# Latent attention in a one-core encoder trunk: query products behind half a projection block, one weight block split on VectorE, projection products ahead of a value product

## The reference

```python
h = x @ w_in
c_q, c_kv, k_rope, dq, dk, dv = jnp.split(h, offs, axis=-1)
q = (rms_norm(c_q, g_q, RMS_EPS) @ w_uq).reshape(b, s, MLA_HEADS, MLA_NOPE_DIM + MLA_ROPE_DIM)
kv = (rms_norm(c_kv, g_kv, RMS_EPS) @ w_ukv).reshape(b, s, MLA_HEADS, MLA_NOPE_DIM + MLA_V_DIM)
...
o_mla = mla_attention(q_nope, q_rope, k_nope, k_rope, v_mla)      # softmax(q k^T) v, per head
o_d = diff_attention(dq[..., 0, :], dq[..., 1, :], dk[..., 0, :], dk[..., 1, :], dv, lam)
```

## Time and profile before

| | |
|---|---|
| median of three runs | 792.22 us (792.11 to 793.13) |
| the profiled execution | 793.97 us |
| its span | 791.9 us |
| busy: PE, PEld | 739.6 us (93%), 614.2 us (78%) |
| busy: DVE, ACT, POOL | 581.1 us (73%), 483.8 us (61%), 269.8 us (34%) |
| granted TensorE clock, mean | 0.975 of full |
| DMA | 179.35 MB, 226 GB/s over the span |

### The profile page before, as it was taken

How to read it: one execution, slowest core, us unless ns; L and a number is a source line. 1 busy time by engine, 2 the same in 40 slices (tenths; PEclk the granted TensorE clock), 3 DMA queues, 4 the chain that set the end, 5 groups by cost and what they waited for, 6 DMA issues and landing times.

```text
span 791.9 us, 12710 instructions
## 1 busy us (share of the span) xinstructions
PE 739.6 (93%) x3844; PEld 614.2 (78%) x3844; DVE 581.1 (73%) x974; ACT 483.8 (61%) x874; POOL 269.8 (34%) x292
## 2 busy tenths in 40 slices
PE   4999989998999699999999899999999999999984
PEld 3898878887888477777788677888877777777862
DVE  6965354556554766686677889998998888888757
ACT  3334354556554656675045267887878888888635
POOL 3132356556654243334421114232222222222111
PEclk9999999999999879999997999999999999999998
DMA  9724310222024863202835759999999999999863
GB/s 342 250 104 134 119 54 27 81 67 67 2 95 155 286 246 120 94 27 80 297 137 200 284 177 392 392 381 388 385 364 382 379 383 365 391 380 375 287 212 159
DMA packets 71484, 179.35 MB, mean 226 GB/s; under 512 B 11687, under 2 KB 28071, under 8 KB 71444
## 3 DMA queue, kind: packets, MB, share of 16 engines
q1 hardware_dynamic: 66692, 166.34, 55.5%
q0 software_dynamic: 4752, 12.51, 6.4%
HBM read 153.20 MB, written 30.42 MB: 232 GB/s over the span
## 4 chain that ended last, share of the span: by engine, by line
PE 57%; DMA 20%; DVE 12%; ACT 5%; issue 3%; POOL 2%; SPq 1%; DVEq 0%; ACTq 0%; POOLq 0%
PE bank L648 33%; DMA rawG<-in_w_gate 16%; PE bank L1774 3%; PE bank L1776 3%; PE bank L1775 3%; DVE eGl L1929 2%; DMA dv_l<-dv_low 2%; PE bank L783 2%; PE bank L1797 1%; PE bank L1796 1%; PE bank L1795 1%; PE bank L2154 1%; ACT eGh L1859 1%; DVE eUl L1929 1%; DVE eDl L1929 1%
## 5 line engine op out<-in xcount | busy, mean ns | idle before, releaser
L1929 DVE TENSOR_TENSOR eDl<-rawD,eDh 128x1024 fp32r<-128x1024 f32 x68 | 80.2, 1220 | 12.6 <-ACT eDh L1859 12.4
L1268 POOL TENSOR_SCALAR me<-me,mrec 128x512 f32<-128x512 f32 (+1 forms) x48 | 64.8, 1354 | 55.9 <-DVE mrec L1447 55.8
L1929 DVE TENSOR_TENSOR eUl<-rawU,eUh 128x1024 fp32r<-128x1024 f32 x68 | 78.8, 1220 | 2.7 <-ACT eUh L1859 2.7
L1929 DVE TENSOR_TENSOR eGl<-rawG,eGh 128x1024 fp32r<-128x1024 f32 x64 | 75.5, 1221 | 6.1 <-ACT eGh L1859 5.1
L2052 POOL DMA_INDIRECT acc_rows<-yg,idx_s x16 | 29.7, 1859 | 133.6 <-ACT yg L1884 133.6
L1859 ACT ACTIVATE eGh<-rawG 128x1024 fp32r<-128x1024 f32 x64 | 65.9, 1059 | 7.6 <-DMA rawG<-in_w_gate 7.1
L1859 ACT ACTIVATE eDh<-rawD 128x1024 fp32r<-128x1024 f32 x64 | 64.0, 1056 | 0.0
L1774 PE MATMUL bank<-eGh,xgT_h 128*128 128x512 f32 x136 | 56.0, 412 | 8.6 <-DVE xgT_l L1934 7.4
L1859 ACT ACTIVATE eUh<-rawU 128x1024 fp32r<-128x1024 f32 x64 | 62.9, 1052 | 0.0
L1774 PE MATMUL bank<-eUh,xgT_h 128*128 128x512 f32 x136 | 54.6, 401 | 0.0
L1776 PE MATMUL bank<-eGl,xgT_h 128*128 128x512 f32 x136 | 53.3, 392 | 0.0
(11 more groups left out here) (345 smaller groups left out, 2186.0 us busy)
## 6 DMA issues: line engine op xcount, KB each, us to landing
rawG<-in_w_gate SPq DMA_DIRECT2D x68, 512.0 KB, 15.6
rawU<-in_w_up SPq DMA_DIRECT2D x68, 512.0 KB, 12.3
rawD<-in_w_down SPq DMA_DIRECT2D x68, 512.0 KB, 13.6
wb_raw<-in_w_in SPq DMA_DIRECT2D x8, 512.0 KB, 4.7
wo_raw<-in_w_o SPq DMA_DIRECT2D x8, 512.0 KB, 7.4
xln_rows<-res SPq DMA_DIRECT2D x6, 512.0 KB, 3.8
dqk_high<-st_h SPq DMA_DIRECT2D x8, 384.0 KB, 2.3
dqk_low<-st_l SPq DMA_DIRECT2D x8, 384.0 KB, 3.3
```

Of the source, the lines that this page charges most:

```text
L1268: nc.gpsimd.tensor_scalar(e, e, mrec[:, g % NSB:g % NSB + 1], None, ALU.mult).then_inc(m_p, 1)
L1929: nc.vector.tensor_tensor(wl_[X][i][:], raw_of(X, t, i)[:], f32(wh_[X][i][:]), ALU.subtract).then_inc(s_lo[X], 1)
```

## The change

- **Start-up, TensorE:** Q(1, 1) stood ahead of the 24 matmuls of B(1, 1); it now stands behind the first 12 of them.
- **Start-up, block 2:** the low part of weight block 2 moves from GpSimd to VectorE, between `reciprocal(1)` and `q_rotated(1, 1)`. Its copy on ScalarE moves up, ahead of `exp(2)`.
- **Start-up, GpSimd:** `normalise(1)` now stands ahead of `q_low(1, 1)`, and the block's subtraction is gone from there.
- **Head 4:** V(1, 2) moves from slot 24 to slot 23, ahead of Q(5, 1). The first part of B(5, 0) moves from slot 26 (7 products) to slot 25 (9 products), where it stands ahead of `scores(29)` and of the value product `product(7)`; slot 27 has 6 instead of 8. The other heads keep the table.

```diff
-    by_vector = [("c", 1)] + [("v", i) for i in range(4)] + [("o", c) for c in range(8)]
+    by_vector = [("c", 1)] + [("v", i) for i in range(4)] + [("b", 2)] + [("o", c) for c in range(8)]
...
-    V_SLOTS = {3 * NT + 2: 0, 3 * NT + 4: 1, 4 * NT: 2}
+    V_SLOTS = {3 * NT + 2: 0, 3 * NT + 4: 1, 3 * NT + 5: 2}
...
     B_PIECES = {2: (0, 0, 0, 7), 3: (0, 0, 7, 15), 5: (0, 0, 15, 17), 0: (-1, 0, 17, 24)}
+    B_PIECES_4 = {1: (0, 0, 0, 9), 3: (0, 0, 9, 15), 5: (0, 0, 15, 17)}
...
-                block_piece(B_PIECES, h, i)
+                block_piece(B_PIECES_4 if h == 4 else B_PIECES, h, i)
...
         scores(2)
+        block_part(1, 1, 0, 12)
         kq_project("Q", 1, 1)
-        block_part(1, 1, 0, 12)
         scores(3)
...
         high(("B", 1, 0))
+        block_weights_high(2)
         exp(2)
         q_high(1, 1)
-        block_weights_high(2)
...
-        for h in range(2):
-            for x in range(2):
-                q_low(h, x)
-                if h == 1:
-                    normalise(x)
-        block_weights_low(2)
+        q_low(0, 0)
+        q_low(0, 1)
+        q_low(1, 0)
+        normalise(0)
+        normalise(1)
+        q_low(1, 1)
...
         reciprocal(1)
+        wait_whigh(dve, ("b", 2))
+        nc.vector.tensor_tensor(wb_l[0][:], wb_raw[0][:], f32(wb_h[0][:]), ALU.subtract).then_inc(s_wlow_v, 1)
         q_rotated(1, 1)
```

## The result

The changed kernel takes 787.16 us, median of 13 runs (784.24 to 790.83), against 792.45 us (791.5 to 796.99, 13 runs) for the kernel before on the same chip: 0.9924 of the time, 95% interval 0.9905 to 0.9943. The forecast was 787.1 and the range 785.2 to 790.0. The profiled execution took 789.17 us with a span of 785.9 (793.97 and 791.9 before): 4.8 less in time, 6.0 in span. The sum of the forecast for this execution was 788.1; the time outside the span, 3.3 us here and 2.1 before, it had taken as fixed.

A forecast was written before the change was run, and what follows sets the result against it. TensorE has no slack inside the attention slots, so its waits ahead of and between them were the target: 793.97 - 3.9 - 2.0 = 788.1 us profiled. Unprofiled 787.9 or 786.3, middle 787.1, range 785.2 to 790.0.

The forecast's parts named there:

- The start of `turn_probs(0)`: Start-up on TensorE: 111.8 instead of 112.89, 1.05 us earlier, worth nothing alone since tile 2 is late by more.
- Hole A: TensorE's waits at the end of the start-up, 0.83 and 2.08 us, plus slowed slot 2: gain 2.3 + 1.6 = 3.9 us.
- the first term: Start-up: `turn_probs(2)` starts at 114.45 instead of 116.73, as `normalise(2)` ends earlier on GpSimd: gain 2.3 us.
- no exclusion: Start-up case: VectorE's block 2 subtraction and GpSimd do not block each other, `probs_low(0)` decides: gain 2.8 us.
- The clock behind it: Slot 2 on TensorE: without the long wait the clock stays full and the 13 matmuls save 1.58 us.
- Hole B: TensorE's 2.14 us wait before `product(7)`: nine products of B(5, 0) fill it, gain 2.0 us, bounds 0 and 2.1.
- To the end: Behind 258 us: semaphores pass the shift on whole; differential attention starts 5.9 us earlier, 4.3 without the old clock fall.
- The middle: Unprofiled median: 787.1 us, between 787.9 (win of 4.3) and 786.3 (win of 5.9).
- Only half: Rival: GpSimd goes first at 109.35 (1.3 instead of 2.3) or head 4's slots stall (0 instead of 2.0); 789.4 us, chance 0.18.
- bound elsewhere: Rival: differential attention or expert stream sets the time, the 4 to 6 us return as waits; 791.5 us, chance 0.07.
- More comes: Rival: a start at another moment shortens the 17 us half-clock stretch by a few us; 784.5 us, chance 0.08.
- Slower: Rival: the differential attention's clock fall is prolonged or a second one starts there; 793.6 to 795.2 us, chance 0.04.

The follow-up runs named there:

- experiment 6: Kernel before with only TensorE's new start-up order, first half of B(1, 1) ahead of Q(1, 1): 794.73 us, one run.
- experiment 5: Changed kernel with TensorE's start-up order as before, Q(1, 1) ahead of the first half of B(1, 1): 789.22 us, one run.
- experiment 2: Kernel before with only the head 4 edits of the change, start-up as before: 792.58 us, ratio 0.9986; run again, 789.18 us.
- experiment 7: Changed kernel with V(1, 2) back in slot 24, block pieces in their new slots: 795.98 us, one run.
- experiment 4: The changed kernel again, unaltered, for a second profile: 787.13 us, ratio 0.9918 to the kernel before.
- experiment 3: Changed kernel plus 7 and 9 unused matmuls before tiles 0 and 1 of the differential attention: 784.39 us, ratio 0.9873 to the kernel before.
- experiment 1: Kernel before with only the start-up edits of the change, head 4 as before: 791.78 us, ratio 0.9968.
- experiment 9: Changed start-up, head 4 edits replaced by block 5's low part on VectorE: 786.15 us, ratio 0.9922 to the kernel before.
- experiment 10: Changed kernel plus block 5's low part on VectorE, q_high(5, 0) ahead of slot 23's V copy, 7 and 9 unused matmuls: 783.00 us, ratio 0.9882 to kernel before.

## Why the prediction was right

**The start of `turn_probs(0)`** was forecast at 111.8 and came at 111.76. That it is worth nothing while GpSimd is late held (experiment 6: -0.35), and that it is worth something afterwards too (experiment 5: 1.1).

**Hole A, tile 2: right in mechanism, mis-sized in one term.** Forecast 114.45, measured 113.86: the first term is 2.79 us (inside one trace) and not 2.3. The term is the meeting of VectorE and GpSimd. The forecast let VectorE wait 0.3 us for the end of `normalise(0)` and then hold `normalise(1)` back until 110.5, to end at 112.05. VectorE did not wait; GpSimd's next operation was lengthened by 0.71 instead and ended at 111.5. The value lands on the bound that was given for no exclusion, 2.8, yet exclusion there was, on GpSimd's side alone: the bound was that of `probs_low(0)`, which was now 0.08 us earlier than GpSimd. The wait left before tile 2 was 0.36 and not about 1 us. Rows that were taken for proof of the succession (the 3.99 us operation at 14.12) showed another VectorE instruction beside another of GpSimd. In the profile of before they are:

```profile
13.28 3.75 POOL L1249 TENSOR_TENSOR wc_l<-wc_raw,wc_h 128x1664 fp32r<-128x1664 f32 x1 [5.70 <-ACT wc_h L992]
19.96 1.28 DVE L1365 SCALAR_TENSOR_TENSOR res<-res,rstd,ln_b 128x1024 f32<-128x1024 f32 x1
```

The operation of 14.12 ended at 18.11, 1.08 us behind the end of GpSimd's TENSOR_TENSOR, and an equally large one alone takes 1.28: that one was held.

The Trainium skill, page "SBUF — State Buffer", section "SBUF: two separate sides", has it that whichever of the two starts first keeps the port pair for its whole instruction. The rows of 13.28 and 14.12 agree. The runs do not agree for the pair of this change: with GpSimd's TENSOR_SCALAR under way VectorE's subtraction ran its usual 1.21 and 1.23 us, started 0.4 and 0.7 us before the other's end. In the other direction, VectorE first, 1.58 became 2.29, as the rule would have it.

**The clock behind it.** Forecast 1.6 (1.58 in the row), measured 4.56 to 3.00, 1.56. But experiment 2, run twice, shows that with the start-up of the kernel before it isn't always paid. The forecast's doubt, whether unprofiled runs had this fall, was the right one; it stays open how many of them do. That the change removes it is better shown: no fall there in any of the ten profiles with the shorter wait.

**Hole B.** Forecast 2.0. The distance gives 6.37 - 2.79 - 1.56 = 2.02, and the step before `product(7)` 2.30 - 0.31 = 1.99. The statement that no wait above 0.3 us would be left before `product(7)` was met by the measure in which it was made (0.15 us idle). That slots 26 and 27 would keep up held, and experiment 7 shows that the cover for it was the earlier V product.

**To the end.** Forecast 5.9 us at the differential attention, measured 6.37 (6.45 by the clock readings, 259.06 and 252.61); then the span is 6.0 shorter, so 0.4 was lost again. A window near the end names one place; it holds later work after the change than before, but before the clock was full over all of 740 to 780 us. Before:

```profile
750.00:760.00 10.00, 7.85 (x36) 6.05 (x34) 4.83 (x6) 5.66 (x7) 3.34 (x4) 1.00 0.47 96
```

After:

```profile
750.00:760.00 10.00, 7.86 (x29) 6.25 (x30) 5.06 (x7) 1.29 (x2) 0.04 (x1) 0.83 0.92 311
```

and in the second execution of the changed kernel (experiment 4):

```profile
750.00:760.00 10.00, 7.75 (x34) 5.64 (x33) 5.18 (x8) 2.12 (x4) 0.64 (x2) 1.00 0.93 302
```

The clock fell there in one execution of the changed kernel and not in the other. From the first differential scores to the end those two took 533.3 and 531.3 us, and the kernel before 532.8: the 0.4 lies within what one kernel varies by, and nothing shows that it belongs to the change. Over the fourteen profiles this part spreads from 528.3 to 536.1 us, with the two that lack the long low stretch at 528.3 and 530.1.

**The median.** The gain of 5.3 us lies between the 4.3 and the 5.9 of the forecast. The middle was a choice without a row behind it, and 787.1 against 787.16 is luck beyond what the working deserved: the tile term was 0.5 too small, and the runs of the changed kernel scatter from 784.2 to 790.8. That scatter goes with the mean clock: of the 13 runs those at 784.2 to 785.5 us have 0.981 to 0.984, those at 788.5 to 790.8 have 0.975 to 0.977. Runs of experiment 3, without the low stretch, have 0.985 to 0.990 and a spread of 4.1 us; those of experiment 4 have 0.974 to 0.984 and a spread of 5.7.

**The rivals.** "Only half" and "bound elsewhere" fall with the 6.37 at the differential attention and the 6.0 at the end. "More comes", by another length of the long low stretch, was the best of them: in the profile of experiment 4 the window of 264 to 281 us has 0.60 where the profiled change had 0.52, and all that lies behind the first differential scores took 2.0 us less at the same slots' distance, in part by the fall near 753 us that it lacks. Experiment 3 shows what the stretch costs, 2.7 us in the medians, where the forecast had put its full price at up to 7.3. "Slower", by a second fall in the differential attention, did not come; falls at a place that had none came in experiments 1 and 7, in the slots, and cost about 1.6 us each.

## What to carry to other kernels

Take a slow low-part subtraction out of the engine whose row is the late one before filling the wait that it causes: both worked here, and at head 4 the first needed no new order on TensorE (experiment 9). An edit that starts an engine earlier is worth nothing until the later of its two conditions has moved, so such edits are measured together and apart. Where TensorE waits a few times in short order ahead of dense work, look at the granted clock of that work; here 16 unused matmuls that fit into the waits brought 2.7 us, and 7 brought nothing. Before taking a difference of two profiles apart, compare the granted clock stretch by stretch: here one kernel's two executions differed by 2.0 us behind the edited part.

## What the runs showed of the hardware

- VectorE's subtraction of two SBUF tiles ran its full speed (1.21 and 1.23 us) beside a GpSimd TENSOR_SCALAR that by its recorded span was still under way for 0.4 and 0.7 us; the GpSimd operation that began beside it took 2.29 us instead of 1.58. VectorE's SCALAR_TENSOR_TENSOR behind a GpSimd TENSOR_TENSOR under way took 3.99 us instead of 1.28.
- Behind the same wait of 2.1 us, with the same instructions on all engines up to there, the clock was at 0.52 in one execution and at 1.00 in two. Behind a wait of 2.16 us at hole B it was at 0.51 in one execution (experiment 1), and behind one of 2.14 us there at 1.00 in the kernel before.
- The stretch of 17 us at half clock in the differential attention (0.50) is neither due to the transfers (DMA share 1.04 with and without it) nor a cost that must be paid: with the waits ahead of it filled the clock was 1.00 over 258 to 400 us (experiments 3 and 10).
